# Whose turn it is to add a row: one of two on VectorE instead of two of three, from the attention on

## The reference, cut to what matters

```python
u = jnp.take(expert_u, it, axis=0)            # tokens x 128 picks x 1024
a = jax.nn.gelu(jnp.einsum('tkd,td->tk', u, ht), approximate=False) * gt
vv = jnp.take(expert_v, it, axis=0)
return jnp.einsum('tk,tkd->td', a.astype(vv.dtype), vv)
```

## Time and profile before

| | |
|---|---|
| median of 3 runs | 3324.57 us (3320.59 to 3329.91) |
| profiled execution, its own time | 3332.64 us |
| span of its instructions | 3330.7 us |
| mean granted clock of PE | 0.904 of full speed |
| busy: PE, DVE, ACT, POOL | 2658.0, 2424.1, 1185.6, 1233.4 us |
| DMA | 1247.23 MB, mean 374 GB/s |

### The profile page before, as it was taken

How to read it: one execution, slowest core, us unless ns; L and a number is a source line. 1 busy time by engine, 2 the same in 40 slices (tenths; PEclk the granted TensorE clock), 3 DMA queues, 4 the chain that set the end, 5 groups by cost and what they waited for, 6 DMA issues and landing times. The chain is left out here.

```text
span 3330.7 us, 29036 instructions
## 1 busy us (share of the span) xinstructions
PE 2658.0 (80%) x8188; PEld 1476.4 (44%) x8188; DVE 2424.1 (73%) x5581; ACT 1185.6 (36%) x3370; POOL 1233.4 (37%) x1085
## 2 busy tenths in 40 slices
PE   5798788768868888788768888788868899777776
PEld 4575544334445443365445444365445444322322
DVE  7775788788877788756976888746967878754544
ACT  1141233358822333313822333314842223323222
POOL 0110245344444445333334444434333345433332
PEclk9899899988788999888778999988768999999999
DMA  8782799999999999999999999999999999999997
GB/s 320 271 288 92 276 420 409 364 360 346 351 381 414 384 421 412 418 386 369 377 374 418 395 421 414 413 376 366 375 357 379 412 402 412 417 422 404 421 421 324
DMA packets 266714, 1247.23 MB, mean 374 GB/s; under 512 B 20117, under 2 KB 106533, under 8 KB 135351
## 3 DMA queue, kind: packets, MB, share of 16 engines
q0 software_dynamic: 156064, 1106.97, 82.2%
q1 hardware_dynamic: 110482, 138.36, 11.6%
q10 hardware_dynamic: 8, 0.06, 0.0%
HBM read 1243.18 MB, written 7.36 MB: 375 GB/s over the span
## 5 line engine op out<-in xcount | busy, mean ns | idle before, releaser
L1554 PE MATMUL psum<-space 128*128 128x512 f32 x3192 | 1618.2, 646 | 411.3 <-ACT space L1598 365.6
L1688 POOL DMA_INDIRECT space<-in_peer_uv,expert x1024 | 1200.6, 1172 | 1833.2 <-PE psum L1554 1170.3
L1629 DVE CUSTOM_DVE_ANT_0 space<-space,h 128x1024 f32<-128x1024 f32 x1024 | 1246.6, 1222 | 655.3 <-DMA space<-in_peer_uv,expert 630.2
L1554 PEld LDWEIGHTS psum<-space 128*128 128x128 f32 x3192 | 618.3, 203 | 1166.0 <-issue 573.9
L1587 ACT ACTIVATE space<-space 128x2 f32<-128x2 f32 x512 | 103.9, 203 | 1492.8 <-DVE space L1629 1482.3
L713 PE MATMUL psum<-space 128*128 128x256 f32 (+2 forms) x1584 | 388.0, 403 | 69.8 <-DMA space<-in_w_in_c 33.1
L713 PEld LDWEIGHTS psum<-space 128*128 128x128 f32 x1584 | 315.2, 202 | 161.2 <-issue 55.0
L1598 ACT ACTIVATE space<-ident,space 128x128 f32<-128x128 f32 x798 | 278.1, 387 | 1.7 <-PE psum L1554 0.2
L1231 PE MATMUL psum<-space 128*128 128x256 f32 x1024 | 263.1, 386 | 13.8 <-DVEq L574 5.3
L1231 PEld LDWEIGHTS psum<-space 128*128 128x128 f32 x1024 | 198.7, 195 | 139.5 <-issue 105.5
L1590 ACT ACTIVATE space<-space,gate 128x1 f32<-128x1 f32 x1024 | 245.6, 287 | 16.8
(11 more groups left out here) (181 smaller groups left out, 1821.9 us busy)
## 6 DMA issues: line engine op xcount, KB each, us to landing
space<-in_peer_w_q SPq DMA_DIRECT2D x32, 1024.0 KB
space<-in_ada_w SPq DMA_DIRECT2D x12, 2048.0 KB, 15.7
space<-in_ada_w POOLq DMA_DIRECT2D x24, 1024.0 KB, 5.6
space<-in_w_in_c SPq DMA_DIRECT2D x24, 1024.0 KB
space<-in_peer_uv,expert POOLq DMA_INDIRECT x1024
space<-in_w_out_ab SPq DMA_DIRECT2D x8, 1024.0 KB
space<-skewed SPq DMA_DIRECT2D x32, 256.0 KB
space<-in_w_out_c SPq DMA_DIRECT2D x8, 1024.0 KB
```

Source lines behind the costliest of these rows:

```text
L1554: last = nc.tensor.matmul(b.bank[part][:, :], b.diag2[:, n % DIAGS, :], b.pairs[:, p % PAIRS, 1, part * BANK:(part + 1) * BANK], start=(p ...
L1629: dve.tensor_tensor_reduce(out=row, in0=row, in1=b.h[:, tile(q), :], scale=1.0, scalar=0.0, op0=ALU.mult, op1=ALU.add, accum_out=b.dots2[: ...
L1688: pool.indirect_dma_start(out=b.pair_rows[q % PAIRS], out_offset=None, in_=ins["peer_uv"], in_offset=bass.IndirectOffsetOnAxis(ap=b.expert ...
```

## The change

The window from `middle` to `end` no longer goes to `thirds`; the window of `halves` reaches to `end` instead. So from the first pick of a window to its end, through attention and the parts behind it, DVE adds the odd picks and PE the even ones. `thirds` stays empty, and `middle` is not used.

```diff
             rest = following[chosen:]
             if attended:
-                halves.append((first + ADD_LAG, middle))
-                thirds.append((middle, end))
+                halves.append((first + ADD_LAG, end))
         done = plan.close()
         sums = Sums(n_picks, halves, thirds)
```

## The result

The changed kernel takes 3383.0 us in the median of 4 runs (3373.8 to 3387.6), the kernel before 3327.2 beside it (4 runs). The ratio is 1.0165, with a 95% interval of 1.0135 to 1.0195. The forecast was 3337.6 and the range ended at 3362: the direction was right, but the kernel became 55.8 us slower, where 13 were forecast: more than four times as much. The profiled execution took 3383.86 us, its span 3382.1, which is 51.4 more than the earlier trace rows.

What follows compares the result with a forecast made beforehand. No single engine was taken as full: DVE, PE and ACT, handing each other work, are all near it, with DMA at 0.93 to 0.96 in attention. Attention +15 and tails -2 give +13 us on 3324.57: 3337.6 us, range 3306 to 3362.

Steps and rivals of the forecast that it cites:

- Counts and places: Windows from attention on: 43 picks move from DVE to PE, 28 in attention and 15 in the tails; ACT gains 43 diagonals.
- the one that priced PE's waits for diagonals: Attention stages: PE's diagonal waits stay at 36.6 us (stages +3) or grow with the picks by 17 (+20).
- the lower part, +15: Attention stages as a whole: +15 us chosen among cases of +3, +20 and +52, as a late engine's waits shrink.
- All other waits vanish: Attention stages: PE's other 63.8 us of idle time, mostly waits for exponentials, go because PE now comes late; stages 537 us.
- the signs: Attention stages, if right: 841 diagonals, PE above 88% busy, POOL waiting longer for PE than DVE, picks 0.05 to 0.15 us slower.
- PE's load: Attention stages: 28 more picks at 2.4 us cost PE 67 us, bringing it from 81% to 94% busy.
- The granted clock: Attention stages: mean granted clock rises from 0.74 to 0.79 to between 0.80 and 0.90, as long matmuls are added.
- The tails: Stretches after each attention stage: PE's idle time covers 39 us of added picks, DVE's relief gains 2 us.
- The relief of DVE: Rival, attention stages: 35.8 us less DVE work lets gathers start sooner, -18 us, 3306.6 us; chance 0.20.
- Nothing moves: Rival: the ring of seven buffers absorbs PE's added picks and DVE's gap, time stays 3324.6 us; chance 0.27.
- PE at the present price: Rival, attention stages: picks cost 80 us, half the other waits stay, +65 less the tails' 2, 3387.6 us; chance 0.05.
- The shorter gather issue: Rival, POOL in the windows: fewer two-input DVE adds shorten gather instructions, 9 us at most, 3315.6 us; chance 0.06.

Runs made afterwards that it cites:

- the pairs shifted: Changed kernel, PE still on even picks, but ACT takes the Gelu of (odd, next even) pairs; 0.9948 of the kernel before.
- The second experiment: Changed kernel with one of two in the attention stages alone, two of three kept in the tails behind them; 1.0137 of the kernel before.

## Why the prediction was wrong

**Counts and places** were right: 43 picks moved, DVE lost 43 adds of 1.28 us, ACT gained 43 diagonals of 386 ns, the loss lies from attention on.

**The step that failed is the one that priced PE's waits for diagonals.** It took them either as constant (36.6 us) or as growing with the number of picks (17 more, 53.5), and then argued that "waits of an engine that becomes the late one shrink", so that a value in the lower part, +15, was taken. They more than doubled, to 79.5 us, and the attention stages grew by 48. The text had the fact: "half of them come later than PE's picks do now". It stood in the list of what moves, with no price and no rival. It could have been weighed in the trace of before, where PE's picks of both parities lie side by side, 30 of each in the attention stages. Each of these waits ends within 0.1 us of the end of a diagonal, and the diagonals come in the order of the picks; given to their picks in this way, 32.3 of the 36.6 us stand before even picks and 4.3 before odd ones. That is 1.08 us for an even pick and 0.14 for an odd one, where the prediction took 0.60 for all. With 88 even picks, an estimate from these two prices is 95 us. At equal counts, the runs with a third on PE say the same: even picks alone mean 53.1 us of such waits and odd ones alone 14.9.

**The other terms of that sum.** "All other waits vanish" was nearly right: 63.8 us became 18.6. Of the signs, 841 diagonals and ACT's longer wait for the transposes came. PE above 88% busy did not (83%), nor did POOL wait longer for PE (79.7 us) than for DVE (88.4), and a pick became 0.39, 0.28 and 0.10 us slower in the three stages, where 0.05 to 0.15 was stated.

**PE's load.** With the 28 picks more, PE's products took 225.4 us instead of 173.8 in the attention stages (101.8 + 56.0 + 67.6 by the groups above), 52 more where 67 were taken. PE's busy share came to 83%, not 94%. PE did become late, but not by its work alone: the 43 us of added waits for diagonals, with the ticks queued behind them, are nearly as large a term as the 50 us of added busy time. With odd picks, where these waits are gone, the same 28 picks leave PE busy 447.9 us, 15 more than before. The right direction came of an incomplete reason, and in that much it was luck: the same picks shared out by the other parity give 0.9913.

**The granted clock** rose clearly only in the third attention stage (0.78 to 0.86); 0.79 became 0.78 and 0.74 became 0.77. Where the waits are gone, with the same number of picks on PE, it is 0.88, 0.83 and 0.89, and PE's busy time is 35.5 us lower. So a part of the loss may come by way of the clock; how much, no run separates. The Trainium skill, "TensorE: Matmul & The Clock Gate", section "What's actually happening", has it that activity releases the throttle. These rows agree: with the pauses gone the clock is higher. The prediction's own reason, that stretches with more matmul work have the higher clock, holds in its rows only for the last stretch; the first tail, with PE busy 64%, has 0.81, the attention stage before it, with 81%, has 0.79.

**The tails** were taken at -2 us and came out at +19 in the profile. PE was busy 206.1 us there instead of 178.5, and DVE's wait for the output products (line 1174) went from 8.9 + 12.4 + 19.5 = 40.8 us to 22.4 + 13.5 + 25.9 = 61.8. So the idle time of PE did not cover the added products in full. PE's waits for diagonals are not what grew: 4.1 + 22.8 + 12.7 = 39.6 us before, 8.5 + 18.6 + 11.3 = 38.4 with the change. Yet with odd picks, just as many, the tails took 277.5 us and these waits 13.9. With the pairs shifted they took 286.0. So most of the growth goes with the turn; by which wait it comes about is not shown. The second experiment gives 13.6 of the 19 back; how much of it is measurable in the whole is open.

**The rivals.** The relief of DVE (-18 us) was hidden. A gain of its size shows at odd picks, where the diagonals come in time: from a third of the rows on PE to a half the ratio goes from 0.9965 to 0.9913, intervals that do not meet, which is 17 us. "Nothing moves" and "PE at the present price" are out; the second had nearly the size (3387.6 us against 3383.0), by terms that did not come: 80 us of products (52 came), half of the other waits kept (18.6 of 63.8 were), and waits for diagonals as before. The shorter gather issue: POOL's instruction fell from 1172 to 1150 ns in the mean (1177.6 us in sum against 1200.6), 23 us of POOL's time over 1024 gathers, with 43 adds fewer. But a third on PE in odd picks, with as many adds as before, has 1141 ns, and a quarter, with 22 adds more, has 1140. So the number of adds does not account for it, and no run here shows that it changed the time. The Trainium skill, "SBUF — State Buffer", section "Who interferes with whom", has a DVE instruction with two SBUF inputs contend with a GpSimd instruction that reads SBUF. The first pair of means agrees with that in direction, the other two do not.

**Open.** Why the stretches ahead of attention are 16 us shorter in the profile of the changed kernel, where nothing was changed, wasn't tested; in one profile each, several of the other kernels show some of it too. Why the first attention stage takes two thirds of the loss wasn't tested either. It has the most picks and ticks, but a pick there lost more as well, 0.39 us against 0.28 and 0.10.

## What to carry to other kernels

Where work is shared out between engines by a pattern, and a producer handles items in groups, the phase of the pattern against the groups can count for more than the shares do: list for each item the turn in which its input is made and the turn in which it is consumed. A fixed program order turns a short wait for one operand into a wait of everything queued behind, and the engine then looks idle, not late. Try the other phase and one more turn of lag before judging a split; here they turned a loss of 1.7% into a gain of 0.5 to 0.9%. Where items of both phases already run side by side, give each wait to its item and sum by phase first: here that split, 32.3 us to 4.3, stood in the trace of before.

## What the runs showed of the hardware that was not expected

Taking most of the columns out of one matmul group lowered the granted clock in the stages to 0.54 to 0.56 (0.78, 0.77 and 0.86 with the full products) and left PE's busy time almost where it was: less work was not less time. An experiment that lightens PE must be read with its granted clock beside it.
